# Two heads side by side in the index scores, scores and values of a mixer, and 128 rows under the gate terms of an attention layer

## What is computed

```python
# layer b, 16 heads of 128, per block of 128 queries
logits = q @ k.T * 128**-0.5 + c[t] - c[s]          # c: cumulative log forget gate of the head
# mixer, sparse attention, 8 heads of 64: which keys a query sees
head_scores = relu(iq @ ik.T * 64**-0.5)            # 8 index heads of 64, one key
scores = sum_h head_scores[h] * w[h];  sel = top_k(scores, 64)
ya = softmax(qa @ ka.T * 64**-0.5 + bias, over sel) @ va
# mixer, latent attention, 8 heads: 64 plain + 32 rotary columns
yb = softmax(([qn, qr] @ [kn, kr].T) * 96**-0.5, causal) @ v
out = (sigmoid(ga) * (ya @ w_a) + sigmoid(gb) * (yb @ w_b)) @ w_out
```

## Time and profile before

| | |
|---|---|
| median of 3 runs | 1857.71 us (1856.68 to 1860.08) |
| the profiled execution | 1859.46 us, of which span 1857.6 us |
| busy: TensorE, weight loads, DVE, ACT, POOL | 1806.4, 1642.6, 1452.4, 1066.9, 316.4 us |
| granted TensorE clock, mean | 0.989 |
| HBM | 182 GB/s over the span, DMA queue of the weights 54.9% of 16 engines |
| softmax part of b, 401 to 515 us | TensorE 111.4 busy, DVE 87.0, ACT 57.6 |
| mixer loop of m0, 1098 to 1197 us | TensorE 96.0 busy, DVE 70.6, ACT 52.0 |
| the same of m1, 1514 to 1613 us | TensorE 97.2 busy, DVE 71.4, ACT 52.9 |

### The profile page before, as it was taken

One profiled execution on the slowest core, in us unless ns is written; L12 is line 12 of the kernel. 1 busy time (PEld: TensorE's weight loads), 2 busy tenths in 40 slices (PEclk: granted clock), 3 DMA queues, 4 the chain that ended last, 5 costly groups with the idle time before them and its releaser, 6 DMA issues.

```text
span 1857.6 us, 31518 instructions
## 1 busy us (share of the span) xinstructions
PE 1806.4 (97%) x11884; PEld 1642.6 (88%) x11884; DVE 1452.4 (78%) x2781; ACT 1066.9 (57%) x2046; POOL 316.4 (17%) x412
## 2 busy tenths in 40 slices
PE   8999999999999999999999999999999999999997
PEld 8989878878899999899997988889998998889996
DVE  8997677887878788889878697687877687687767
ACT  5887565555554444478765455455555555455554
POOL 1997000000000000089830000020000200020000
PEclk9999999999999999998999999999999999999998
DMA  6444459865558888543454553446764443446552
GB/s 223 137 134 141 146 168 313 274 214 169 170 184 288 297 290 292 197 154 122 132 167 159 183 203 103 148 153 199 238 205 159 148 148 102 148 153 205 189 183 78
DMA packets 92743, 339.66 MB, mean 183 GB/s; under 512 B 10288, under 2 KB 10672, under 8 KB 91952
## 3 DMA queue, kind: packets, MB, share of 16 engines
q1 hardware_dynamic: 92592, 337.64, 54.9%
HBM read 336.55 MB, written 1.05 MB: 182 GB/s over the span
## 4 chain that ended last, share of the span: by engine, by line
PE 67%; DVE 16%; ACT 8%; issue 6%; POOL 2%; DMA 1%; SPq 0%; DVEq 0%; ACTq 0%; POOLq 0%
PE ps L103 65%; DVE wl L119 5%; ACT tmp L109 3%; DVE ps L129 3%; POOL B L119 2%; DVE B L119 2%; PE ps L106 2%; ACT wh L112 2%; DVE tmp L119 1%; ACT B L109 1%; DVE B L124 1%; ACT XS L112 1%; ACT ps L109 1%; ACT os L112 1%; DVE X L129 0%
## 5 line engine op out<-in xcount | busy, mean ns | idle before, releaser
L103 PE MATMUL ps<-XS,wh 128*128 128x256 f32 x4464 | 825.5, 287 | 8.5 <-DVE wl L119 7.5
L103 PEld LDWEIGHTS ps<-XS,wh 128*128 128x128 f32 x4464 | 703.5, 192 | 18.6 <-issue 9.0
L119 DVE TENSOR_TENSOR wl<-raw,wh 128x1024 fp32r<-128x1024 f32 x481 | 590.8, 1256 | 144.9 <-ACT wh L112 143.8
L103 PE MATMUL ps<-XS,wl 128*128 128x256 f32 x2232 | 633.3, 284 | 0.0
L112 ACT CAST wh<-raw 128x1024 fp32r<-128x1024 f32 x481 | 485.7, 1044 | 144.0 <-PE ps L103 137.8
L103 PEld LDWEIGHTS ps<-XS,wl 128*128 128x128 f32 x2232 | 429.4, 192 | 0.1
L119 POOL TENSOR_TENSOR B<-B,tmp 128x237 f32<-128x237 f32 (+11 forms) x384 | 274.7, 758 | 670.3 <-ACT tmp L109 670.3
L103 PE MATMUL ps<-wh,os 128*128 128x512 f32 x864 | 283.9, 394 | 9.1 <-DVE os L119 6.8
L129 DVE SCALAR_TENSOR_TENSOR ps<-B,C,ps 128x254 f32<-128x254 f32 (+16 forms) x544 | 211.8, 469 | 16.9 <-ACT ps L109 16.1
L103 PEld LDWEIGHTS ps<-wh,os 128*128 128x128 f32 x864 | 162.4, 188 | 47.7 <-DVE os L119 10.9
L103 PE MATMUL ps<-B,raw 128*128 128x256 f32 x832 | 191.1, 391 | 0.0
(11 more groups left out here) (152 smaller groups left out, 1737.2 us busy)
## 6 DMA issues: line engine op xcount, KB each, us to landing
raw<-in_w SPq DMA_DIRECT2D x628, 512.0 KB, 4.5
B<-in_ln SPq DMA_DIRECT2D x4, 1024.0 KB, 7.5
C<-in_cst SPq DMA_DIRECT2D x1, 1102.5 KB, 10.3
X<-in_x SPq DMA_DIRECT2D x2, 512.0 KB, 5.8
out_x<-X SPq DMA_DIRECT2D x4, 256.0 KB, 2.5
cb<-in_cb SPq DMA_DIRECT2D x1, 512.0 KB, 13.0
pos<-in_pos SPq DMA_DIRECT2D x1, 160.0 KB, 2.3
raw<-in_w SPq DMA_DIRECT2D x1, 128.0 KB, 3.1
```

Of the source, the lines that this page charges most:

```text
L103: return NOTHING if self.e is None else self.e.matmul(*a, **k)
L119: return NOTHING if self.e is None else self.e.tensor_tensor(o, a, b, op)
```

## The change

In b, `terms` and `choice` span 128 partitions instead of 32; ACT clears `terms` once, and DVE waits for that before it writes the 32 rows that count. In the mixers, index heads come in pairs without a wait between the two, over four banks; the masks of heads n and n+1 go before the scores of both; values come in pairs at odd n; DVE takes the maxima of both heads at even n; `tmp` rotates over four buffers.

```diff
     def b_terms(self):
-        return YS[0:32, 0, 0:384], YS[0:32, 1, 0:16]
+        return YS[:, 0, 0:384], YS[:, 1, 0:16]
...
-            pe.matmul(b[:, 0:384], choice[:, h:h + 1].to_broadcast([32, 128]), terms, start=True, stop=False)
+            pe.matmul(b[:, 0:384], choice[:, h:h + 1].to_broadcast([128, 128]), terms, start=True, stop=False)
...
+        act.activation(terms, self.c("cmask", 0, 384), ACT.Identity, scale=0.0).then_inc(s["evac"].up("terms"), 1)
         act.wait_ge(*s["soft"]["b", "y"])
...
+        dve.wait_ge(*s["evac"]["terms"])
         dve.tensor_copy(terms[:, 128:384], ncs).then_inc(s["soft"].up(("b", "upper")), 1)
...
+        def index_pair(h):
+            pe.wait_ge(*s["evac"][M, "ik"])
+            pe.wait_ge(*s["evac"][M, "iq", 1])
+            if h >= 4:
+                pe.wait_ge(*s["evac"][M, "index", h - 3])
+            index_head(h)
+            index_head(h + 1)
-        index_head(0)
-        index_head(1)
+        index_pair(0)
+        index_pair(2)
         self.unit(pe, ps[5][:, 0:T], f"{M}.ckv", M)
-        for h in range(2, 8):
-            index_head(h)
+        index_pair(4)
         for n in range(4):
+            if n == 1:
+                index_pair(6)
...
-            if n < 16:
+            if n < 2:
+                masked(n)
                 scores(n)
+            elif n < 16 and n % 2 == 0:
+                masked(n)
+                masked(n + 1)
+                scores(n)
+                scores(n + 1)
             if n >= 2:
                 pe.wait_ge(*(s["rope"][M, "q", 5] if n == 2 else s["turned"][M, n - 3]))
-                self.pe_turn(pe, self.tmp[2 + (n - 2) % 3], 6, (M, n - 2))
+                self.pe_turn(pe, self.tmp[2 + (n - 2) % 4], 6, (M, n - 2))
...
-            if n >= 2:
-                h, x = (n - 2) % 8, n - 2
+            if n >= 3 and n % 2:
...
+                pe.wait_ge(*s["turned"][M, n - 2])
+                for x in (n - 3, n - 2):
+                    h, V = x % 8, VA if x >= 8 else VM
+                    self.pe_value(pe, V[:, 0, 64 * h:64 * h + 64], V[:, 1, 64 * h:64 * h + 64], self.tmp[2 + x % 4], 7,
+                                  slice(64 * (h % 2), 64 * (h % 2) + 64), (M, x))
...
-                if n >= 3:
-                    act.wait_ge(*s["value"][M, n - 3])
+                if n >= 4:
+                    act.wait_ge(*s["value"][M, n - 4])
...
         for n in range(18):
+            for x in (n,) if n < 2 else (n, n + 1) if n < 16 and n % 2 == 0 else ():
+                maxima(x)
             if 1 <= n < 17:
-                self.dve_quotients(dve, self.tmp[2 + (n - 1) % 3], self.stat(n - 1), (M, n - 1))
+                self.dve_quotients(dve, self.tmp[2 + (n - 1) % 4], self.stat(n - 1), (M, n - 1))
```

More of the change, by code:

```diff
@@ L1347, in act_b @@
             self.feed_act(act, f"b.v0.{kp}")
+        terms, choice = self.b_terms()
+        act.activation(terms, self.c("cmask", 0, 384), ACT.Identity, scale=0.0).then_inc(s["evac"].up("terms"), 1)
         act.wait_ge(*s["soft"]["b", "y"])
@@ L1394, in act_b @@
             if j == 1:
-                terms, choice = self.b_terms()
-                act.copy(choice, self.c("pair", 0, 16, rows=slice(0, 32))).then_inc(s["evac"].up("choice"), 1)
+                act.copy(choice, self.c("pair", 0, 16)).then_inc(s["evac"].up("choice"), 1)
                 self.act_masks(act)
@@ L1436, in dve_b @@
         y, e1, lf, cc, ncs = self.b_rows()
-        terms, choice = self.b_terms()
+        terms = self.b_terms()[0][0:32]
         self.dve_residual(dve, "a0")
@@ L1892, in index_head @@
         def index_head(h):
-            b = ps[2 + h % 2]
+            b = ps[h % 4]
             q = slice(64 * (h % 2), 64 * (h % 2) + 64)
[L1895 to L1898, removed]
             pe.matmul(b[:, 0:128], IQ[q, h // 2, 0:128], IK[q, 0:128], start=True, stop=True)
@@ L1913, in pe_m @@
                     pe.wait_ge(*s["square"][M, "lat"])
+                    pe.wait_ge(*s["evac"][M, "index", 7])
                     self.token_sum(pe, 0, 0, self.tmp[0][:, 0:T], True, False)
@@ L1963, in pe_m, with masked @@
                 s["gemm"].up((M, "uv", tb)), 1)
-        def scores(n):
+        def masked(n):
             h, b = n % 8, ps[4 + n % 2]
@@ L1970, in scores @@
             if n >= 8:
+                pe.wait_ge(*s["select"][M, "sel"])
+            pe.matmul(b[:, 0:384], idn, chosen if n >= 8 else causal, start=True, stop=False)
+        def scores(n):
+            h, b = n % 8, ps[4 + n % 2]
+            if n >= 8:
                 q = slice(64 * (h % 2), 64 * (h % 2) + 64)
                 pe.wait_ge(*s["evac"][M, "qk", 3])
-                pe.wait_ge(*s["select"][M, "sel"])
-                pe.matmul(b[:, 0:384], idn, chosen, start=True, stop=False)
                 pe.matmul(b[:, 0:128], QA[q, h // 2, 0:128], KA[q, h // 2, 0:128], start=False, stop=False)
@@ L1981, in scores @@
                 pe.wait_ge(*s["evac"][M, "kr"])
-                pe.matmul(b[:, 0:384], idn, causal, start=True, stop=False)
                 pe.matmul(b[:, 0:128], QM[q, h, 0:128], KM[q, h, 0:128], start=False, stop=False)
@@ L2065, in index_head @@
                 act.wait_ge(*s["select"][M, "index", h - 4])
-            act.activation(self.tmp[2 + h % 4][:, 0:384], ps[2 + h % 2][:, 0:384], ACT.Relu, scale=0.125).then_inc(
+            act.activation(self.tmp[2 + h % 4][:, 0:384], ps[h % 4][:, 0:384], ACT.Relu, scale=0.125).then_inc(
                 s["evac"].up((M, "index", h)), 1)
-        index_head(0)
-        index_head(1)
+        for h in range(4):
+            index_head(h)
         self.feed_act(act, f"{M}.ckv")
         ev(v["CKV"], 5, s["gemm"][f"{M}.ckv"], (M, "ckv"))
-        for h in range(2, 8):
+        for h in range(4, 6):
             index_head(h)
@@ L2077, in act_m @@
             self.feed_act(act, f"{M}.qk{2 * n + 1}")
+            if n == 1:
+                index_head(6)
+                index_head(7)
             dst, k = (v["QA"], v["KA"])[n // 2], n % 2
@@ L2268, in dve_m, with maxima @@
             dve.tt(v["QM"][rr, h, :], v["QM"][rr, h, :], q, ALU.add).then_inc(s["rope"].up((M, "q", h)), 1)
-        for n in range(18):
[L2270 to L2288, removed]
+        def maxima(n):
+            h = n % 8
+            st, b = self.stat(n), ps[4 + n % 2][:, 0:384]
+            dve.wait_ge(*s["score"][M, n])
+            if n >= 8:
+                q = self.tmp[n % 2][:, 0:384]
+                dve.wait_ge(*s["evac"]["bias", 5])
+                if n >= 10:
+                    dve.wait_ge(*s["exps"][M, n - 2])
+                dve.stt(q, b, 0.125, self.bias_views()[0][:, h, :], ALU.mult, ALU.add).then_inc(
+                    s["soft"].up((M, "s", n)), 1)
+                dve.wait_ge(*s["soft"][M, "s", n])
+            else:
+                q = b
+            dve.reduce_max(st[:, 0:1], q[:, 0:128])
+            dve.reduce_max(st[:, 1:2], q[:, 128:384]).then_inc(s["soft"].up((M, "red", n)), 1)
+            dve.wait_ge(*s["soft"][M, "red", n])
+            dve.ts(st[:, 2:4], st[:, 0:2], -1.0 if n >= 8 else -(96.0 ** -0.5), None, ALU.mult, None).then_inc(
+                s["soft"].up((M, "max", n)), 1)
```

13 lines of the change are left out of this document (5 added, 8 removed).

## The result

The change takes the kernel from a median of 1857.31 us (4 runs) to **1833.68 us** (4 runs, 1829.08 to 1834.95): ratio 0.986, interval 0.984 to 0.988. I had said 1830, 1826 to 1841.

What follows compares the result with a forecast made beforehand. TensorE's stream was taken as the bound. A mixer saves 1.77 + 3.76 + 6.16 + 0.38 - 0.2 = 11.87 us, two 23.7, with b 28.5; that makes 1829, stated as 1830 us, range 1826 to 1841.

Steps and rivals of the forecast that it cites:

- What bounds it: Whole kernel: TensorE, busy 1806 of 1857.6 us; time falls only if its own stream shortens or its waits go.
- Gate terms: Layer b: gate matmuls over 128 rows instead of 32 save 0.30 us a head, 4.8 us in all.
- Index heads: Mixers, ahead of the loop: index heads in pairs take 3.50 us instead of 5.27, saving 1.77 us a mixer.
- Sparse scores: Mixer loop: four pairs of sparse heads, each 1.30 us instead of 2.24, save 3.76 us a mixer.
- Values: Mixer loop: the second head of a pair is free, 0.88 us saved; seven pairs give 6.16 us a mixer.
- The last pair: End of the mixer loop, heads 14 and 15: gains 0.38 us, not 0.88, as head 15's transposes wait.
- New waits: Mixer loop: late quotients lose 0.8 and 0.5 us, the 1.1 wait for bank 7 goes; net -0.2 a mixer.
- Columns in order: Rival, values: the second head waits for the first, each pair saves only 0.23 us; 1839 us, chance 0.27.
- Pace of DVE and ACT: Rival, mixer loop: DVE's 1.27 us waits for casts stay unfilled, 9 us lost; 1838 us, chance 0.07.
- Nothing beside anything: Rival, whole change: no new work runs side by side, only changes of shape saved, some 13 us; 1845, chance 0.02.
- slower case: Rival, mixer loop: at each even n TensorE waits for the odd head's exponentials before either mask; 1863 us, chance 0.03.
- The signs: Expected in the profile: value groups of eight busy about 0.9, b's mask following after 0.17, DVE's cast waits well below 22.7.

Runs made afterwards that it cites:

- values_same_half: The changed kernel with the odd head's values sent to the same 64 array columns as the even head's; 1842.11 us, 0.991 of before.
- both_moves: The changed kernel with the odd head's quotients between the two maxima on DVE and the third branch product (bf4) one step later; 1824.88 us, 0.984 of before.
- both_moves_again: The kernel of both_moves, unchanged, measured once more; 1826.24 us, 0.983 of before.

## Why the prediction was right, and where it was not

The time (1830 for 1834) and the forecast, pairs that run at once, were right. The sum was 28.5, the parts measure 24.2. The terms that missed missed on the same side, so 1830 lies near not because errors cancelled but because the terms that carry the sum (3.76 and 6.16 a mixer) held.

- **What bounds it.** Right. All that was gained came from TensorE's stream: its busy time fell by 32.6 us, that of DVE by none.
- **Gate terms, 4.8 forecast, 3.8 measured.** A head in the middle of b gains 0.28 and not 0.30, so the size a head was right. Its split wasn't: the start of the gate term came 0.17 earlier (I said 0.10), and the mask still comes 0.26 behind the gate term, not 0.17. The 0.20 that I gave to the 32 rows there was half something else, which no run took apart. And heads 0 and 1 gave 0.5 back to waits: I had cover for the clearing, and none in the sum for waits that are there anyway.
- **Index heads, 1.77 forecast, 1.57 measured.** No wait for DVE ate it. Of the 0.2 that is missing, half is one term: the second of two pairs in a row, which I put at 0.65, costs 0.75 (four heads take 1.61 from start to start, two take 0.86). The other 0.1 is a term that the sum left out. The change has three groups of index heads between units where there were two, and in m1 the unit behind a group takes 2.97, one behind a unit 2.88.
- **Sparse scores, 0.94 a pair.** Mask, mask and scores take 1.29 (0.43 + 0.86) and not 2.23: 0.94, exact.
- **Values, 0.88 a pair.** The step "the second head is free" was right, from a row that showed row halves only: 0.87 at each of seven pairs, 0.78 of it passes and 0.09 the change of shape behind one unit. The last pair, 0.38 forecast: its values save 0.75 (0.77 and 0.79 before, 0.81 now), but the six transposes take 2.07 where 1.22 and 0.30 stood before, 0.55 lost; 0.20 is left. Over a loop the values bring 7 x 0.87 + 0.20 = 6.3 against 6.54.
- **New waits, net -0.2 forecast, -1.7 measured.** This step failed most. I found the mechanism, quotients of the odd head behind another head's maxima, and priced it at two places (0.8 and 0.5). It stands at nearly every pair (at head 3 in either order of DVE's queue). Against the 2.95 of a unit with no wait behind it, the unit ahead of the odd transposes takes 1.12 more at head 1, 0.26 at head 3, 0.01 at head 5 and 0.35 to 0.37 at each of the four from head 7 on. That is 2.85 a mixer, against the 1.18 of bank 7. The mistake was to ask only whether DVE keeps up over a pair of steps. It does, and still the quotients are late within the pair, since the transposes that want them come one unit after the scores that release the maxima ahead of them.
- **Sum of a loop:** 3.76 + 6.3 - 1.7 = 8.4, measured 8.47 and 8.52, against 10.1.
- **The rivals.** Columns in order (0.27) fell to the timeline (0.81 for eight passes), and values_same_half shows what it would have cost: 1842, where I had 1839. Pace of DVE and ACT (0.07): its waits of 1.27 were mostly filled, as said (12.6 for 22.7). Nothing beside anything (0.02) fell to the same rows; its parts add up to 12, not 13. The slower case (0.03): TensorE never waited for the odd head's exponentials ahead of the masks.
- **The signs.** Groups of eight, 0.9 busy, DVE's waits below 22.7: seen. Mask 0.17 after the gate term: not seen. "A wait for quotients at each pair" was named as a sign of being wrong. It came at six of seven pairs, and cost 1.5 us a loop more than the sum had, not the gain.

## What to carry to other kernels

Put heads that use half of the array next to each other with no wait between them, in both kinds of halves: the second head cost a hundredth of a microsecond here. Then look for who used to be covered by the work that shrank: after grouping, ask of each instruction in the group not whether its supplier keeps up on average but when, counted from the event that releases the supplier, it is wanted. A queue order that puts the urgent piece (quotients) between two that can wait (maxima) gave back 4.5 us for an edit of a few lines. And where TensorE's stream has two units in one place and none in another, move one: 1.4 us a loop.

## What the runs showed of the hardware

- Matmuls of two column halves that write the same PSUM bank run at once: eight passes in 0.81 us from start to start, 1.45 if both heads use one half. By the trace's single records the eight passes start in four twos, 13 or 14 ns apart within each two (in all sixteen pairs of the two mixers, and likewise in the sparse scores). A record doesn't say whose pass it is, but the two that report a head's values as done stand in the last two. So the second head's passes don't wait for those of the first that stand ahead of them; in order, eight could not fit into the time of four. The Trainium skill (TensorE: Matmul & The Clock Gate, Part 3) has matmuls strictly in the order of the program, and these runs disagree.
- Four index heads in a row (sixteen passes, busy 1.68) take 1.61 from start to start, so a second pair of row halves costs 0.75 behind the first.
- Changing from column halves to row halves directly costs no more than changing from column halves to full shape: 0.81 for the values in both cases.
- A DVE subtraction can be held up for 10 us where GpSimd works. The profiled run of both_moves, 22 us above its median, had three subtractions that took 9.7, 10.4 and 10.6 us where the same three take 1.6 in both_moves_again. One of them in DVE's timeline, and TensorE's waits for weight pieces over the whole span (8.9 is the longest, 8.7 the total in both_moves_again):

```profile
82.48 9.71 DVE L119 TENSOR_TENSOR wl<-raw,wh 128x1024 fp32r<-128x1024 f32 x1
```

```profile
PE ps L103 <- DVE wl L119: 26.9, 18, 8.9
```

All three lie outside the edited code (at 82, 805 and 857 us), and no other profile of this study has one; the longest subtraction in any of them takes 2.3. All three lie where GpSimd (POOL) is at work, and there the two hold each other up: in each of before, after and both_moves_again 30 subtractions meet a GpSimd product of the convolution, with a median of 1.5 where the others have 1.2, and the only 30 of the 384 products above 1 us are ones that meet a subtraction (about 1.6, the others 0.7). In the slow three GpSimd ran on at 0.7 for 13 to 15 products. The first two subtractions ended with the first long product (1.61 at 91.12, 1.68 at 814.24), the third 1.09 after GpSimd's last (866.67). These rows fit a subtraction that waits until GpSimd lets it in. No run took GpSimd away to show it, and why it came first so often in this one execution stays open.
